# First mixer: the decays' chain reordered on every engine, norm powers in four pieces, masked product and last value tile moved

## The chip, the cores and the metric

One NeuronCore of a Trainium2 chip runs the whole program in one launch. The metric is the device time in microseconds, the median of the runs. The engines: TensorE (PE) multiplies, VectorE (DVE), ScalarE (ACT) and GpSimd (POOL) do elementwise work, SyncE (SP) issues the DMAs.

## What is computed

1024 tokens with 1024 features pass through a first block (a gated delta rule mixer, GDN, then a gated linear attention mixer, each with residual and layer norm) and a second one (windowed attention and sparse latent attention, then a feed-forward network). The change touches the GDN mixer only. It has 8 heads, keys of 128, values of 256, and works in chunks of 64 tokens:

```python
qkv = causal_conv_silu(p[..., :GDN_QKV], conv_w)        # p = x @ w_in, 4 taps, then silu
q, k = l2norm(q), l2norm(k)                             # t * rsqrt(sum(t*t) + 1e-6)
beta = sigmoid(b_logit); g = -exp(a_log) * softplus(a_logit + dt_bias)
gc = cumsum(g)                                          # within a chunk
decay = where(causal, exp(gc_i - gc_j), 0)
A = where(strict, (k*beta) k^T * decay, 0)
u, w = solve(A + I, [v*beta, k*beta*exp(gc)])           # unit lower triangular
qk = (q k^T) * decay
# scan over chunks: v_new = u - w S; o = (q*exp(gc)) S + qk v_new; S = S*g_last + k_dec^T v_new
# then o * rsqrt(mean(o*o) + 1e-6) * norm_w * silu(gate), and the product with w_out
```

## The kernel before

**Groups and tiles.** The mixer runs over 4 groups of 2 heads. A group projects 12 tiles of 128 output columns by 1024 tokens: 0 and 1 are q, 2 and 3 k, 4 to 7 v, 8 to 11 the gate. A tile is 48 matmuls of 128x512 (8 pieces of the contraction, 2 halves of the tokens, 3 products of high and low parts; `half`, lines 630, 631, 633). The raw weights of a tile come by DMA into one buffer; ScalarE rounds out the high part (`split`, line 1338), VectorE subtracts it for the low part (`split`, line 1951), and the next load waits for that. Two pairs of part buffers alternate, so the high part of tile i + 2 waits for the matmuls of tile i.

**Convolution.** ScalarE writes the first product from PSUM into one of two accumulators (`conv_first`, line 1352), VectorE adds three taps (`tap`, line 1962), ScalarE takes the silu (`conv_last`, line 1357). For q and k ScalarE squares (line 1361) and TensorE sums over the features by 8 products with one column of ones (`squares`, line 661), tile i into columns 8i to 8i + 7 of PSUM bank 6. For v TensorE turns the tile (`turn_values`, line 668) into the pair of banks 4 and 5, and VectorE scales it with beta into `vtok` (`values`, line 1969). For a gate tile ScalarE writes a silu (`gate`, line 1365).

**Scales.** When all four squares are there, VectorE's `scalars` adds 1e-6 (line 2008), GpSimd raises all 32 columns to -0.5 (line 2739), and VectorE makes the scales of A, of the keys and of the outputs (lines 2010 to 2016, event `sc`).

**Decays.** For each n of 8 pairs of chunks `decay` goes round the engines: GpSimd multiplies the triangle U with g (line 2667, `rU`); TensorE sums it over rows (line 692, `rB`); VectorE subtracts gc (line 2023, `rr`, which waits for `sc`); ScalarE takes exp (line 1410, `ex`); GpSimd zeroes the upper part (line 2672, `D`); TensorE has made k k^T and k q^T (lines 697, 699, `kk`); VectorE scales them (lines 2031, 2036: `B`, `qkT`); TensorE transposes B (line 707, `bT`), and ScalarE copies it, scaled, as A (lines 1420, 1421).

**Inverse.** `tee` inverts four n at a time by levels of masks: VectorE masks A (line 2047, `am` 0), writes I - that (line 2050) into `XX`, TensorE transposes it (line 721, `x0`), VectorE writes I - x0 (line 2054, `x1`); then for levels 1 to 6 TensorE multiplies the masked A (line 731), ScalarE copies the product into `Wb` (line 1432), TensorE multiplies again (lines 743, 745), and VectorE subtracts (lines 2063 to 2069). GpSimd makes the masked A of levels 1 to 5 (line 2686). TensorE uses banks 4 to 7 here. `XX` lies where accumulator 0 is; `Wb` and the mask buffer of even levels, `Am[0]`, lie where accumulator 1 is.

**Order.** Each engine has its own program, and an order is written out by hand: a yield is a place at which the other generator goes on. All engines follow the same two functions:

```python
def gdn_order(g, tiles, decay, tee, before_scan, scan_step):
    def four(q):
        for n in range(4 * q, 4 * q + 4):
            yield from decay(g, n)
    v_steps = tiles(g, range(5, 9))
    for _ in range(3):
        next(v_steps)
    interleave([four(0), v_steps])
    tee(g, 0)
    interleave([four(1), tiles(g, range(9, 12), True)])
    tee(g, 1)
```

`interleave` takes one step of each in turn until both are through. On TensorE `tiles` yields after 6, 9, 15 (9 and the 6 of the next half) and 9 matmuls of a tile, four times a tile; the convolution of tile i - 1 goes with the projection of tile i. `decay` yields four times for n < 4 and three times for n >= 4. `place_` takes the next PSUM bank of a ring and waits until its last tenant is emptied.

Of the kernel before, what the change touches and what calls it, by code (L numbers as in the profile page):

```python
# [166 lines left out]
def program(nc, I, out):  # L167
    ctx = ExitStack()
    with ctx:
# [86 lines left out]
        Am = [shared[:, 1536 + i * 512:2048 + i * 512] for i in range(2)]  # L256
# [4 lines left out]
        oT_odd = flat_masks[:, 448:960]  # L261
        sm = cutter(small, 832)
# [5 lines left out]
        rqk = sm(32)  # L268
# [201 lines left out]
        def gdn_order(g, tiles, decay, tee, before_scan, scan_step):  # L470
            def four(q):
                for n in range(4 * q, 4 * q + 4):
                    yield from decay(g, n)

            v_steps = tiles(g, range(5, 9))
            for _ in range(3):
                next(v_steps)
            interleave([four(0), v_steps])
            tee(g, 0)
            interleave([four(1), tiles(g, range(9, 12), True)])  # L480
            tee(g, 1)
            before_scan(g)
            for n in range(10):
                scan_step(g, n)
# [112 lines left out]
        def pe_program(e):  # L597
# [59 lines left out]
            def squares(g, i):  # L657
                sqb = bank[6]
                pe.wait_ge(("sq", g, i), ("ones",))
                for n in range(8):  # L660
                    m = mm(sqb[:, i * 8 + n:i * 8 + n + 1], accs[i % 2][:, n * 128:(n + 1) * 128], ones[:, 0:1], True, True)
                m.then_inc(*did("sqs", g, i))

            def turn_values(g, i):
                b = place_(R["v"], ("vT", g, i), ("v", g, i))
                pe.wait_ge(("s", g, i), ("ident",))
                for n in range(8):
                    m = tr(b[:, n * 128:(n + 1) * 128], accs[i % 2][:, n * 128:(n + 1) * 128], ident)
                m.then_inc(*did("vT", g, i))
# [18 lines left out]
            def decay(g, n):  # L688
# [13 lines left out]
                if n < 4:  # L702
                    yield
# [137 lines left out]
            for g in range(4):  # L841
                R["p"], R["v"], R["f"], R["r"] = Ring([1, 0] if g else [0, 1], True), Ring([2], True), Ring([0, 1]), Ring([6, 7])
                R["n"], R["k"] = Ring([4, 5]), Ring([2, 3])
                place_(Ring([6]), ("sqb", g), ("rqk", g))
# [476 lines left out]
        def act_program(e):  # L1321
# [45 lines left out]
            def tiles(g, some, last=False):  # L1367
                for i in some:
                    if i < 11:
                        split(12 * g + i + 1)  # L1370
                    if i - 1 < 8:
                        conv_first(g, i - 1)
                    else:
                        gate(g, i - 1)
                    yield from blank(4)
                    if i - 1 < 8:
                        conv_last(g, i - 1)
                    if i - 1 < 4:
                        square(g, i - 1)
                if last:  # L1380
                    gate(g, 11)
# [25 lines left out]
            def decay(g, n):  # L1407
# [4 lines left out]
                if n < 4:  # L1412
                    yield
# [11 lines left out]
            def tee(g, q):  # L1425
                ac.wait_ge([("vT", g, 6), ("vT", g, 7)] if q == 0 else None)
# [502 lines left out]
        def dve_program(e):  # L1929
# [42 lines left out]
            def tiles(g, some, _=False):  # L1972
                for i in some:
                    if i < 11:
                        split(12 * g + i + 1)
                    yield
                    for s_ in range(1, 4):
                        if i - 1 < 8:
                            tap(g, i - 1, s_)
                        yield  # L1980
                    if 4 <= i - 1 < 8:
                        values(g, i - 1)
# [20 lines left out]
            def scalars(g):  # L2003
# [3 lines left out]
                dv.wait_ge([("sqs", g, i) for i in range(4)], ended(g))  # L2007
                ts(rqk, bank[6][:, 0:32], 1e-6, None, ALU.add).then_inc(*did("rqk", g))
                dv.wait_ge(("rqp", g))
# [8 lines left out]
            def decay(g, n):  # L2018
# [20 lines left out]
                if n < 4:  # L2039
                    yield  # L2040

            def tee(g, q):
# [3 lines left out]
                dv.wait_ge([("A", g, n) for n in ns], ("d", "masks"), [("w", g, n - 4, 4) for n in ns] if q else [("vT", g, 6), ("vT", g, 7)])  # L2046
                tt(am, A8, tri[:, 0, :].unsqueeze(1).to_broadcast([128, 8, 64]), ALU.mult).then_inc(*did("am", g, q, 0))
                for c, n in enumerate(ns):
                    dv.wait_ge(("am", g, q, 0), ("xw", g, n - 4, 6) if q else None)
                    stt(XX[:, c, 0:2, :], am[:, 2 * c:2 * c + 2, :], -1.0, ident2.unsqueeze(1).to_broadcast([128, 2, 64]),  # L2050
                        ALU.mult, ALU.add).then_inc(*did("x0d", g, n))
                for c, n in enumerate(ns):
                    dv.wait_ge(("x0", g, n))
                    stt(XX[:, c, 2:4, :], at("x0", g, n)[:, 0:128].rearrange("p (j c) -> p j c", j=2), -1.0,
                        ident2.unsqueeze(1).to_broadcast([128, 2, 64]), ALU.mult, ALU.add).then_inc(*did("x1", g, n))
                for l in range(1, 7):
# [114 lines left out]
            for g in range(4):  # L2171
                if g == 0:
# [9 lines left out]
                    for s_ in range(1, 4):  # L2182
                        tap(0, 0, s_)
                        tap(0, 1, s_)
                    run(tiles(g, [3, 4]))
                    rates()
                    decays()
                else:
                    split(12 * g + 1)
                    for i in range(1, 5):  # L2190
                        split(12 * g + i + 1)
                        for s_ in range(1, 4):
                            tap(g, i - 1, s_)
                scalars(g)
                gdn_order(g, tiles, decay, tee, skip, scan_step)
# [437 lines left out]
        def pool_program(e):  # L2633
# [30 lines left out]
            def decay(g, n):  # L2664
# [3 lines left out]
                i_.then_inc(*did("rU", g, n))  # L2668
                yield
# [6 lines left out]
                if n < 4:  # L2676
                    yield

            def tee(g, q):
                ns = range(4 * q, 4 * q + 4)  # L2680
                A8 = kd_a.rearrange("p (x c) -> p x c", x=8)
                po.wait_ge([("A", g, n) for n in ns], ("d", "masks"), [("vT", g, 6), ("vT", g, 7)])
# [54 lines left out]
            for g in range(4):  # L2737
                po.wait_ge(("rqk", g))
                tt(rqk, rqk, cm05[:, 0:32], ALU.pow).then_inc(*did("rqp", g))
# [537 lines left out]
```

## Time and profile before

| | |
|---|---|
| median of 3 runs | 3395.48 us (3391.42 to 3397.43) |
| the profiled execution | 3392.56 us, span 3390.8 us |
| granted TensorE clock, mean | 0.978 |
| TensorE busy | 3214.0 us, 95% of the span |
| VectorE, ScalarE, GpSimd busy | 50%, 35%, 16% |
| group 1 of the first mixer | its first projection matmul starts at 323.80 us |

How to read it: on an engine, instructions run in the order of its program, and an instruction that waits holds up all behind it. Matmuls are pipelined: a 128x512 one is shown with 0.39 us and the next starts 0.23 us later. PEclk is the granted clock as a share of 2.4 GHz: 1.00 is 2.4 GHz, and at its lower level the engine runs at 1.2 GHz. The first groups differ from each other only at their start and end, so group 1 is shown for all.

### The profile page before, as it was taken

The numbers are of one execution on the slowest core, as the hardware profiler recorded it, in microseconds if no ns is written. First come the engines' busy times: TensorE is split into PE (matmuls) and PEld (weight loads), VectorE is DVE, ScalarE is ACT, GpSimd is POOL, SyncE is SP. The second block draws the span as 40 slices with busy tenths as digits, with TensorE's granted clock in tenths as the row PEclk, the third lists the DMA queues.
The fourth block names the chain that finished last, engine by engine and source line by source line (L and its number), as shares of the span: only waits on it lengthen the run. The fifth ranks groups of instructions, "written<-read, shape, count | busy, mean of one in ns | idle before, by whom it ended". The sixth has DMA issues, their size and how long they took to land.

```text
span 3390.8 us, 48503 instructions
## 1 busy us (share of the span) xinstructions
PE 3214.0 (95%) x19989; PEld 2658.8 (78%) x19989; DVE 1697.1 (50%) x3474; ACT 1202.8 (35%) x2403; POOL 533.8 (16%) x785
## 2 busy tenths in 40 slices
PE   8999999999999989899889999999999999999998
PEld 6778878877887767787767788778888788888886
DVE  3444445354444645545563799576643333234234
ACT  4442344244344433423353232466732311111113
POOL 0220112022012423203262132000110000000000
PEclk9999999999999989999989999999999999999999
DMA  2113102201220021132112132100042311111111
GB/s 103 38 39 114 42 20 76 87 27 44 100 87 33 32 72 51 49 104 88 53 65 77 38 106 82 56 1 1 1 174 100 131 38 62 38 50 50 50 50 50
DMA packets 59479, 210.12 MB, mean 62 GB/s; under 512 B 7015, under 2 KB 11721, under 8 KB 54522
## 3 DMA queue, kind: packets, MB, share of 16 engines
q1 hardware_dynamic: 59258, 207.02, 17.7%
q8 instruction: 157, 2.57, 0.3%
q14 instruction: 64, 0.52, 0.0%
HBM read 161.91 MB, written 45.09 MB: 61 GB/s over the span
## 4 chain that ended last, share of the span: by engine, by line
PE 85%; DVE 5%; ACT 4%; POOL 3%; issue 2%; DMA 1%; SPq 0%; POOLq 0%; DVEq 0%; ACTq 0%
PE pp L630 11%; PE pp L631 10%; PE pp L633 10%; PE pp L1237 9%; PE pp L1238 8%; PE pp L1239 8%; PE pp L803 2%; PE pp L805 2%; PE pp L804 2%; PE pp L1210 2%; PE pp L1194 2%; PE pp L731 1%; PE pp L761 1%; PE pp L745 1%; PE pp L743 1%
## 5 line engine op out<-in xcount | busy, mean ns | idle before, releaser
L630 PE MATMUL pp<-gx_hi,pw_hi 128*128 128x512 f32 x1504 | 617.0, 410 | 20.3 <-DVE pw_lo L1951 20.3
L633 PE MATMUL pp<-gx_hi,pw_lo 128*128 128x512 f32 x1504 | 595.8, 396 | 0.0
L631 PE MATMUL pp<-gx_lo,pw_hi 128*128 128x512 f32 x1504 | 594.8, 396 | 0.0
L630 PEld LDWEIGHTS pp<-gx_hi,pw_hi 128*128 128x128 f32 x1504 | 288.0, 191 | 86.0 <-DVE pw_lo L1951 20.7
L633 PEld LDWEIGHTS pp<-gx_hi,pw_lo 128*128 128x128 f32 x1504 | 287.2, 191 | 63.2
L631 PEld LDWEIGHTS pp<-gx_lo,pw_hi 128*128 128x128 f32 x1504 | 287.9, 191 | 55.4
L1237 PE MATMUL pp<-mix_hi,wt_hi 128*128 128x512 f32 x704 | 274.1, 389 | 2.8 <-DVE arena L2596 1.6
L1238 PE MATMUL pp<-mix_lo,wt_hi 128*128 128x512 f32 x704 | 273.9, 389 | 0.0
L1239 PE MATMUL pp<-mix_hi,wt_lo 128*128 128x512 f32 x672 | 261.4, 389 | 0.0
L1924 ACT ACTIVATE xT<-pp 128x1024 f32<-128x1024 f32 x22 | 22.6, 1029 | 535.4 <-PE pp L1239 535.4
L2628 DVE TENSOR_TENSOR xT<-xT,pp 128x1024 f32<-128x1024 f32 x22 | 26.9, 1221 | 368.8 <-ACT xT L1924 368.8
L1951 DVE TENSOR_TENSOR pw_lo<-arena,pw_hi 128x1024 fp32r<-128x1024 f32 x68 | 83.6, 1230 | 231.3 <-ACT pw_hi L1338 231.3
L1237 PEld LDWEIGHTS pp<-mix_hi,wt_hi 128*128 128x128 f32 x704 | 132.1, 188 | 30.6 <-DVE arena L2596 1.8
L1238 PEld LDWEIGHTS pp<-mix_lo,wt_hi 128*128 128x128 f32 x704 | 132.1, 188 | 27.4
L1239 PEld LDWEIGHTS pp<-mix_hi,wt_lo 128*128 128x128 f32 x672 | 126.1, 188 | 26.2
L2615 DVE TENSOR_TENSOR y_ffn<-y_ffn,pp 128x512 f32<-128x512 f32 x176 | 115.7, 684 | 57.3 <-PE pp L1239 56.5
L2886 POOL TENSOR_SCALAR small<-small 128x1 f32<-128x1 f32 x16 | 3.0, 190 | 821.9 <-ACT xT L1846 723.1
L1237 PE MATMUL pp<-wt_hi,a_hi 128*128 128x512 f32 x336 | 132.1, 393 | 0.0
L1238 PE MATMUL pp<-wt_lo,a_hi 128*128 128x512 f32 x336 | 131.0, 390 | 0.0
L1239 PE MATMUL pp<-wt_hi,a_lo 128*128 128x512 f32 x336 | 130.8, 389 | 0.0
L2421 DVE TENSOR_SCALAR_CACHE_REDUCE xT<-y,small 128x656 bf16<-128x656 f32 (+1 forms) x124 | 128.5, 1092 | 0.0
L1338 ACT ACTIVATE pw_hi<-arena 128x1024 fp32r<-128x1024 f32 x68 | 71.6, 1054 | 156.4 <-PE pp L633 119.2
(507 smaller groups left out, 6808.9 us busy)
## 6 DMA issues: line engine op xcount, KB each, us to landing
arena<-in_tiles_dram SPq DMA_DIRECT2D x73, 512.0 KB, 3.6
arena<-in_units_dram SPq DMA_DIRECT2D x33, 1024.0 KB, 4.8
y_scratch<-y SPq DMA_DIRECT2D x48, 512.0 KB, 2.9
y<-y_scratch SPq DMA_DIRECT2D x40, 512.0 KB, 4.6
xT<-in_tiles_dram SPq DMA_DIRECT2D x27, 512.0 KB, 4.0
xT<-in_w_outs_dram SPq DMA_DIRECT2D x12, 1024.0 KB, 7.2
arena<-gates_scratch SPq DMA_DIRECT2D x16, 512.0 KB, 3.4
xT<-in_wall_dram SPq DMA_DIRECT2D x3, 2048.0 KB, 10.0
```

Source lines behind the costliest of these rows:

```text
L630: mm(b[:, hs], wh[:, c], X[0][:, k, hs], k == 0, False)
L631: m = mm(b[:, hs], wh[:, c], X[1][:, k, hs], False, both and k == 7)
L633: m = mm(b[:, hs], wl[:, c], X[0][:, k, hs], False, k == 7)
L803: mm(b, hi[:, t, :], wh, t == 0, False)
L804: mm(b, hi[:, t, :], wl, False, False)
L1237: mm(o, l[0][:, c], r[0][:, d], first, False)
L1238: mm(o, l[0][:, c], r[1][:, d], False, False)
L1239: return mm(o, l[1][:, c], r[0][:, d], False, last)
L1338: act(parts(u)[0], tile_place[u], ACT.Copy).then_inc(*did("ph", u))
L1951: tt(lo, tile_place[u], hi.bitcast(F32), ALU.subtract).then_inc(*did("pl", u))
L2421: i_ = ts(vis[i], work[i], thr[:, i - 1:i] if bit < 31 else 0.0, None, ALU.is_ge, ALU.add, accum_out=count[:, i - 1:i])
L2615: tt(yv, yv, at("dn", j, n, hf), ALU.add).then_inc(*did("yd", j, n, hf))
```

## The change

- The powers of the norms are made by tiles: VectorE's `norm_piece` adds 1e-6 to 8 columns, GpSimd's `power` raises 8 columns, and `scales` (the rest of `scalars`) is called in `gdn_order` after the first three steps of the value tiles. The squares of tile i lie in bank 6 + i % 2. GpSimd's `sums` for n = 0 (line 2667) is made ahead of the fourth power.
- `decay` has the additional yield for n < 2 only, on all four engines.
- `Am[0]` lies in the second half of the masks' buffer (the place of `oT_odd`, used in the scan), so the masked product waits for A and no longer for the value tiles.
- The last value tile is turned into the ring of the projections; VectorE scales value tile 6 one step later, in the next tile's first step, and tile 7 in `tee` behind line 2054.
- VectorE makes the low parts of tiles 9, 10 and 11 after the first yield of a tile instead of ahead of it.
- ScalarE makes gate tile 8 and the high part of tile 10 at the head of `tee` instead of behind it, and the silu of tile 7 one step earlier.

```diff
 Wb = shared[:, 1024:1536].rearrange("p (c e) -> p c e", c=4)
-Am = [shared[:, 1536 + i * 512:2048 + i * 512] for i in range(2)]
 halves = (slice(0, 64), slice(64, 128))
...
 oT_odd = flat_masks[:, 448:960]
+Am = [oT_odd, shared[:, 2048:2560]]
 sm = cutter(small, 832)
...
-def gdn_order(g, tiles, decay, tee, before_scan, scan_step):
+def gdn_order(g, tiles, decay, tee, before_scan, scan_step, scales=None):
     def four(q):
...
         next(v_steps)
+    if scales:
+        scales(g)
     interleave([four(0), v_steps])
...
     def squares(g, i):
-        sqb = bank[6]
+        sqb = place_(Ring([6 + i % 2]), ("sqs", g, i), ("rqk", g, i))
         pe.wait_ge(("sq", g, i), ("ones",))
...
     def turn_values(g, i):
-        b = place_(R["v"], ("vT", g, i), ("v", g, i))
+        b = place_(R["p" if i == 7 else "v"], ("vT", g, i), ("v", g, i))
         pe.wait_ge(("s", g, i), ("ident",))
...
         yield
-        if n < 4:
+        if n < 2:
             yield
...
         R["n"], R["k"] = Ring([4, 5]), Ring([2, 3])
-        place_(Ring([6]), ("sqb", g), ("rqk", g))
         R["d"] = Ring([6, 7])
...
     def tiles(g, some, last=False):
         for i in some:
-            if i < 11:
+            if i < 11 and i != 9:
                 split(12 * g + i + 1)
...
                 conv_first(g, i - 1)
-            else:
+            elif i != 9:
                 gate(g, i - 1)
-            yield from blank(4)
+            yield from blank(3 if i == 8 else 4)
             if i - 1 < 8:
...
         yield
-        if n < 4:
+        if n < 2:
             yield
...
     def tee(g, q):
-        ac.wait_ge([("vT", g, 6), ("vT", g, 7)] if q == 0 else None)
+        if q == 0:
+            gate(g, 8)
+            split(12 * g + 10)
+            ac.wait_ge(("vT", g, 6), ("vT", g, 7))
         for l in range(1, 7):
...
     def tiles(g, some, _=False):
         for i in some:
-            if i < 11:
+            if i < 8:
                 split(12 * g + i + 1)
             yield
+            if i == 8:
+                values(g, 6)
+            if 8 <= i < 11:
+                split(12 * g + i + 1)
             for s_ in range(1, 4):
...
                 yield
-            if 4 <= i - 1 < 8:
+            if 4 <= i - 1 < 6:
                 values(g, i - 1)
...
     def rates():
...
-    def scalars(g):
+    def norm_piece(g, i):
+        c = slice(8 * i, 8 * i + 8)
+        dv.wait_ge(("sqs", g, i), ended(g))
+        ts(rqk[:, c], at("sqs", g, i)[:, c], 1e-6, None, ALU.add).then_inc(*did("rqk", g, i))
+
+    def scales(g):
         def two(a):
...
-        dv.wait_ge([("sqs", g, i) for i in range(4)], ended(g))
-        ts(rqk, bank[6][:, 0:32], 1e-6, None, ALU.add).then_inc(*did("rqk", g))
-        dv.wait_ge(("rqp", g))
+        dv.wait_ge([("rqp", g, i) for i in range(4)])
         ts(rqk[:, 0:16], rqk[:, 0:16], 128.0 ** -0.5, None, ALU.mult).then_inc(*did("rqs", g))
...
         yield
-        if n < 4:
+        if n < 2:
             yield
...
     def tee(g, q):
...
         A8 = kd_a.rearrange("p (x c) -> p x c", x=8)
-        dv.wait_ge([("A", g, n) for n in ns], ("d", "masks"), [("w", g, n - 4, 4) for n in ns] if q else [("vT", g, 6), ("vT", g, 7)])
+        dv.wait_ge([("A", g, n) for n in ns], ("d", "masks"), [("w", g, n - 4, 4) for n in ns] if q else ended(g))
         tt(am, A8, tri[:, 0, :].unsqueeze(1).to_broadcast([128, 8, 64]), ALU.mult).then_inc(*did("am", g, q, 0))
         for c, n in enumerate(ns):
-            dv.wait_ge(("am", g, q, 0), ("xw", g, n - 4, 6) if q else None)
+            dv.wait_ge(("am", g, q, 0), ("xw", g, n - 4, 6) if q else ("vT", g, 6))
             stt(XX[:, c, 0:2, :], am[:, 2 * c:2 * c + 2, :], -1.0, ident2.unsqueeze(1).to_broadcast([128, 2, 64]),
...
                 ident2.unsqueeze(1).to_broadcast([128, 2, 64]), ALU.mult, ALU.add).then_inc(*did("x1", g, n))
+        if q == 0:
+            values(g, 7)
         for l in range(1, 7):
...
                 tap(0, 1, s_)
+            norm_piece(g, 0)
+            norm_piece(g, 1)
             run(tiles(g, [3, 4]))
+            norm_piece(g, 2)
             rates()
+            norm_piece(g, 3)
             decays()
...
                 split(12 * g + i + 1)
+                if i >= 2:
+                    norm_piece(g, i - 2)
                 for s_ in range(1, 4):
                     tap(g, i - 1, s_)
-        scalars(g)
-        gdn_order(g, tiles, decay, tee, skip, scan_step)
+        if g:
+            norm_piece(g, 3)
+        gdn_order(g, tiles, decay, tee, skip, scan_step, scales)
...
-    def decay(g, n):
+    def sums(g, n):
         po.wait_ge(("gg",), ("U",), ("bT", g, n - 1) if n else ended(g))
...
         i_.then_inc(*did("rU", g, n))
+
+    def power(g, i):
+        c = slice(8 * i, 8 * i + 8)
+        po.wait_ge(("rqk", g, i))
+        tt(rqk[:, c], rqk[:, c], cm05[:, c], ALU.pow).then_inc(*did("rqp", g, i))
+
+    def decay(g, n):
+        if n:
+            sums(g, n)
         yield
...
         yield
-        if n < 4:
+        if n < 2:
             yield
...
     def tee(g, q):
...
         A8 = kd_a.rearrange("p (x c) -> p x c", x=8)
-        po.wait_ge([("A", g, n) for n in ns], ("d", "masks"), [("vT", g, 6), ("vT", g, 7)])
+        po.wait_ge([("A", g, n) for n in ns], ("d", "masks"), ended(g))
         for l in range(1, 6):
...
     for g in range(4):
-        po.wait_ge(("rqk", g))
-        tt(rqk, rqk, cm05[:, 0:32], ALU.pow).then_inc(*did("rqp", g))
+        for i in range(3):
+            power(g, i)
+        sums(g, 0)
+        power(g, 3)
         gdn_order(g, lambda g_, some, last=False: blank(4 * len(some)), decay, tee, skip, scan_step)
```

## Rows read from the trace of the kernel before

**Rows 1.** The page, busy time of each engine (share of the span) and instructions

```profile
PE 3214.0 (95%) x19989; PEld 2658.8 (78%) x19989; DVE 1697.1 (50%) x3474; ACT 1202.8 (35%) x2403; POOL 533.8 (16%) x785
```

**Rows 2.** TensorE's waits, 0 to 1130 us: us in total, times, longest

```profile
PE pp L707 <- DVE arena L2031: 14.6, 8, 1.9
...
PE pp L721 <- DVE arena L2047: 10.0, 4, 2.5
PE pp L668 <- ACT arena L1357: 8.8, 4, 2.2
...
PE pp L692 <- POOL arena L2667: 1.2, 1, 1.2
```

**Rows 3.** Timeline of TensorE, group 1, start of decays: start us, length us

```profile
383.74 1.84 PE L661 MATMUL pp<-consts,arena 128*128 128x1 f32 x16
...
392.65 0.67 PE L692 MATMUL pp<-arena,consts 128*128 128x256 f32 x2
...
397.95 0.39 PE L633 MATMUL pp<-gx_hi,pw_lo 128*128 128x512 f32 x1
400.56 1.09 PE L668 MATMUL pp<-consts,arena 128*128 128x128 f32 x8 [2.23 <-ACT arena L1357]
```

**Rows 4.** Timelines of the other engines in the same stretch

```profile
378.54 1.06 ACT L1361 ACTIVATE arena<-arena 128x1024 f32<-128x1024 f32 x1
...
385.89 5.42 POOL L2739 TENSOR_TENSOR small<-small,consts 128x32 f32<-128x32 f32 x1 [73.38 <-DVE small L2008]
...
393.27 3.90 DVE L1962 SCALAR_TENSOR_TENSOR arena<-pp,small,arena 128x1023 f32<-128x1023 f32 x3
...
398.16 1.28 ACT L1357 ACT_TABLE_LOAD   x1
399.45 1.06 ACT L1357 ACTIVATE arena<-arena 128x1024 f32<-128x1024 f32 x1
```

**Rows 5.** GpSimd's groups by form, whole run: busy us, mean ns

```profile
L2660 POOL TENSOR_TENSOR small<-small,consts 128x8 f32<-128x8 f32 x2 | 3.3, 1672 | 0.2
```

**Rows 6.** Timeline of VectorE, group 1, ahead of the first inverse

```profile
443.56 1.22 DVE L1969 TENSOR_TENSOR arena<-pp,small 128x1024 f32<-128x1024 f32 x1 [5.30 <-PE pp L668]
444.70 0.60 DVE L2031 SCALAR_TENSOR_TENSOR arena<-pp,small,arena 128x128 f32<-128x128 f32 x2
```

**Rows 7.** Timeline of TensorE, group 1, start of the first inverse

```profile
442.49 1.04 PE L668 MATMUL pp<-consts,arena 128*128 128x128 f32 x8
445.45 0.41 PE L707 MATMUL pp<-consts,arena 128*128 128x128 f32 x2 [1.92 <-DVE arena L2031]
448.35 1.97 PE L721 MATMUL pp<-consts,arena 64*64 64x64 f32 x32 [2.49 <-DVE arena L2047]
450.43 1.97 PE L731 MATMUL pp<-arena 64*64 64x64 f32 x32
...
454.37 1.14 PE L731 MATMUL pp<-arena 64*64 64x64 f32 x32
...
457.21 1.14 PE L731 MATMUL pp<-arena 64*64 64x64 f32 x32
```

**Rows 8.** Timeline of ScalarE, group 1, behind the first inverse

```profile
469.56 1.01 ACT L1365 ACTIVATE xT<-pp 128x1024 f32<-128x1024 f32 x1
```

**Rows 9.** The page, DMA issues: KB each, median us to landing

```profile
arena<-in_tiles_dram SPq DMA_DIRECT2D x73, 512.0 KB, 3.6
```

**Rows 10.** Busy time in stretches: PE PEld DVE ACT POOL, PEclk, DMA share, GB/s

```profile
402.00:406.00 4.00, 4.00 (x12) 3.13 (x12) 4.00 (x7) 0.46 (x1) 0.00 (x0) 0.61 0.24 59
...
985.00:990.00 5.00, 5.00 (x20) 4.12 (x18) 4.12 (x7) 1.47 (x2) 0.00 (x0) 0.66 0.13 26
...
690.00:700.00 10.00, 7.82 (x41) 6.22 (x40) 5.96 (x10) 6.52 (x12) 1.60 (x3) 1.00 0.17 54
```

**Rows 11.** Timelines, group 1, fifth decay step

```profile
486.10 1.23 DVE L1951 TENSOR_TENSOR pw_lo<-arena,pw_hi 128x1024 fp32r<-128x1024 f32 x1 [5.57 <-ACT pw_hi L1338]
...
487.99 0.41 PE L707 MATMUL pp<-consts,arena 128*128 128x128 f32 x2 [1.72 <-DVE arena L2031]
```


## The prediction

> **What bounds the kernel now.** I read the page's busy times first: TensorE is busy for 95% of the span [rows 1], so only time in which it stands still, or runs at the lower clock, can be won. Next the waits of TensorE over the first mixer (0 to 1130 us of the trace), longest first [rows 2]: the transposes of the decay matrices (line 707) waited 14.6 us in 8 places for VectorE's line 2031, the first product of the inverse (line 721) 10.0 us in 4 places for line 2047, the value transposes (line 668) 8.8 us in 4 places for ScalarE's silu, and line 692 once, 1.2 us, for GpSimd. That is 34.6 us, in the same three places in each of the four groups (group 0 has the 1.2 besides). Everything between these places is back to back. The reader is to see that each place is a chain through other engines that begins too late, not an engine without capacity; the timelines of group 1 show which link is late.
>
> **Place 1, the start of the decays.** TensorE issues its last matmul of tile 5 at 397.95 and the value transpose only at 400.56 [rows 3]. With the pace of 0.23 us per matmul, 2.38 us are lost from issue to issue (the wait of 2.23 is counted from the modelled end). Back along the chain [rows 4]: the silu at 399.45 follows a table load of 1.28 us, and this follows exp and subtraction behind the three taps of VectorE that began at 393.27, which were queued behind the scales, which waited for the power on GpSimd, 5.42 us from 385.89. **The change** cuts the power into four pieces of 8 columns. A power of that shape takes 1.67 us [rows 5], against 5.42 for 32 columns. Three pieces run while tiles are still projected, and the last starts at about 385.9. VectorE does the split and two taps of tile 4 before it waits for it: from 385.7, 1.2 and 2.6 us, thus 389.5, by when the power (387.6) is done; were a piece as dear as the whole it would be done at 391.3, still early enough. So the scales are no longer in front of the taps' data. What is late next is the first row sum of the decays, which TensorE issues at 392.65 [rows 3] in its own order and has at 393.3: subtraction and exp 1.0 (from the taps' end at 397.17 to the table load at 398.16 [rows 4]), table load 1.28, silu 1.06, thus about 396.6, against 398.2, when TensorE wants it. The stall goes with 1.6 us to spare. **Gain: 4 x 2.38 = 9.5 us.** In group 0 the row sum also waits for its multiplied mask on GpSimd, behind the power: 1.2 by the wait, 1.3 from issue to issue. The mask now goes before the last power. Against it stands one new hop: the fourth piece's bank is the one that the cumulative sums (line 654) use next, so they wait for VectorE's small addition. No row shows that hop; it lies between 0 and the 0.60 us of a pair of VectorE operations on 256 columns [rows 6]; I take 0.4, as a single addition on 8 columns is nearer to the upper end only by its two handovers. Net 0.9.
>
> In every group VectorE now also waits for the squares before the taps of the next tile. The squares hold TensorE for 1.84 us [rows 3] behind the tile's last matmul, while the taps in any case wait for ScalarE's first product, a pass like the square's 1.06 us [rows 4]; a tap chain starts up to 1 us later. Cover: the square of tile 3 ends at 379.6 [rows 4], 4.1 us before TensorE asks for it at 383.74. Costed at nothing; without that cover it would be 1 us a tile, 12 us in all.
>
> **Place 2, the start of the inverse.** In group 1 [rows 7] the transposes of the last value tile begin at 442.49 and take 0.88 to issue (to 443.37); then 445.45 the last decay transpose, 448.35 line 721, 450.43 the first line 731. So 7.06 us pass between the value tile and line 731. Why [rows 6]: VectorE did the last value tile (1.22 us at 443.56) ahead of line 2031 at 444.70, and the transpose waited for that; behind the transpose come the scaled copies on ScalarE and the masked product on VectorE. **The change** shortens the chain by one step for n = 2 and 3 (14 steps for 14 pieces of TensorE's tiles instead of 16), so the last decay transpose is issued before the last 9 matmuls and the value transposes; it puts the last value tile behind line 2054, and the masked product into a buffer that does not wait for the values. Chain from the decay transpose to line 731: 450.43 - 445.45 = 4.98 us, which I keep. TensorE now fills the first 0.24 + 9 x 0.227 + 0.88 = 3.16 us of it. The value tile to line 731 is then 4.98 - 3.16 = 1.82 us, and the transpose's 0.24 lies in front: 7.06 - 1.82 - 0.24 = **5.0 us a group, 20.0 us**. Of the 1.82, 1.0 is line 721's own work and 0.8 a stall that stays.
>
> The covers, counted from the end of tile 7: value transposes 0.9, values 6 on VectorE until 2.5, split until 3.6, taps until 8.0 with line 2023 of n = 3 between them, line 2031 at 8.6; TensorE asks for it at 11.4. Silu 7 is done at 9.6 and needed at 13.7. The mask of n = 3 on GpSimd needs 1.2 us after a transpose and has 2.0. On ScalarE the gate of tile 8 and the high part of tile 10 now stand ahead of the inverse's copies, about 1 us each, as gate 8's 1.01 [rows 8]: from the end of tile 8 (13.9) until 15.9, and the first copy is wanted at 16.9. Tile 10's load is issued once the low part of tile 9 is there (3.6), and lands in 3.6 us [rows 9], at about 7.5. VectorE's last value tile, 1.22 us behind line 2054, ends about 0.2 us after the first product wants its subtraction; the next round absorbs that. Bank 4 to 7: the last value tile now sits in the tiles' pair, so tile 9 waits for gate 8 (done 15.0, wanted after 40), tile 10 for values 7 and tile 11 for gate 9, all early.
>
> **The clock.** After this stall line 721 and the first line 731 take 1.97 us instead of the 1.14 of the next, and from the first to the second round 3.94 us pass, against 2.84 from the second to the third [rows 7]: 1.1 us a group at half clock. If TensorE works on, **4.4 us** come back. In groups 1 and 3 the granted clock also fell behind place 1, to 0.61 over 4 us and 0.66 over 5 us [rows 10]: 4 x 0.39 and 5 x 0.34, **3.2 us**. Bounds for both together: nothing (it falls elsewhere) to 7.6. I take them whole, as each fall follows a stall that goes. But group 2 had the same stall in 690 to 700 us and kept a clock of 1.00 [rows 10]: whether a stall costs the clock is chance. The Trainium skill (TensorE: Matmul & The Clock Gate, "Part 1: The HAM clock gate") says that a monitor sets the clock by how busy the array was recently, on a count of its own that doesn't start anew with the kernel. By that rule a stall elsewhere can meet a bad moment as well after the change, and the sum would be smaller by the 3.2; by it the trace's one group without a fall beside two with one is as expected.
>
> **Place 3, the fifth decay step.** TensorE waited 1.72 us before 487.99 [rows 11]; with the 0.16 us by which a matmul's modelled end lies behind the issue of the next (0.39 against 0.23), 1.88 us lost. VectorE's line 2031 stood behind the split of tile 11 (486.10 [rows 11]), which waits for ScalarE's high part and this for tile 9's end. In the new order VectorE does each split of these tiles after the first yield, thus behind line 2031. The copies of ScalarE stay behind gate 9 as before, and TensorE's next decay transpose comes 7 us later. **4 x 1.88 = 7.5 us.** No edit touches SyncE's program; its tile loads follow the low parts, at most 1.2 us later each, against the 11 us of a tile's 48 matmuls.
>
> **Sum.** 9.5 + 0.9 + 20.0 + 4.4 + 3.2 + 7.5 = 45.5 us. The profiled execution took 3392.6 us, the median of the runs is 2.9 above it. 3392.6 - 45.5 = 3347.1, as a median 3350. The rest of the kernel (from about 1085 us on) is the same instructions and moves as a block.
>
> **Rivals.**
> - *The clock does not come back (0.13).* The 0.8 us that stay, followed by thin 64x64 products, could leave the half-clock stretch where it is. For: the rows show it right there. Against: the third round, with the same thin products, runs at full speed [rows 7]. Gain 45.5 - 7.6 = 37.9: 3358.
> - *The short steps are too short (0.17).* For n = 2 and 3 there is one piece of TensorE less between the row sum and the transpose. If exp and silu with their table loads, or GpSimd's mask, are late, place 2 gives up about 2.5 us a group, and some stall comes in the middle: 45.5 - 10 - 2 = 33.5: 3362.
> - *Slower (0.04).* The inverse's copies now stand behind the high part of tile 10 on ScalarE, which waits for that tile's load. Place: between gate 8 and line 1432. The load has 14.9 - 3.6 = 11.3 us. Beyond that each us costs one in each group; from 23 us on the whole 45.5 are gone (4 x 11.4), and with 25 us it would be 3403. Against: loads land in 3.6 us, in the median.
> - *It does nothing that counts (0.04).* The gains are taken back in the scan, if that waits for loads or rows: 3395. Against: no such wait over 1 us in TensorE's list.
>
> **Numbers.** Forecast 0.62, rivals as given. Faster by over 0.2% (6.8 us, about what a measurement of this kernel can tell from no change) 0.92, within it 0.04, slower 0.04. Low end: the 0.8 us stalls go too (3.2), and the half-clock stretch at the end of the inverse shrinks, some 6 us: 3340. High end: both middle rivals in part together, 3371.
>
> **What would show it.** Right: in TensorE's waits lines 707 and 668 gone, line 721 gone and in its place about 0.8 us before line 731 in each group; four small powers of about 1.7 us per group; line 731 of the first round in 1.1 us. Wrong: a wait of line 707 for line 2031 in the first four steps (second rival), clock of 0.7 at the inverse's start (first), or ScalarE's line 1338 waiting for a load before the inverse (third).

## The result

The changed kernel takes 3352.0 us (3351.6 to 3355.1), against 3393.8 us for the kernel before on the same chips: a ratio of 0.9879 (95% interval 0.9865 to 0.9893), 41.8 us. The forecast was 3350, the range 3340 to 3371. The profiled executions have spans of 3390.8 and 3350.0 us, 40.8 us apart, against 45.5 worked out. "Before" and "after" below are these two profiles; the other runs are named by what they undo.

TensorE's waits in the first mixer (0 to 1110 us; us in total, times, longest), which answer to [rows 2]:

```profile
PE pp L632 <- DVE pw_lo L1955: 14.4, 1, 14.4
PE pp L736 <- DVE arena L2080: 7.6, 23, 0.4
...
PE pp L733 <- DVE arena L2065: 2.2, 4, 0.6
...
PE pp L656 <- DVE small L2014: 0.3, 1, 0.3
```

The lines that led [rows 2] are gone: no wait of 709 (707 before), 723 (721), 670 (668) or 694 (692) is left. New are 0.56 us before the first line 733 in each group, and the hop of group 0 at line 656, 0.26 us. What waits besides (line 736 at the inverse's last level, the weights of tile 0) waited before as well.

The start of the decays in group 1, timelines of TensorE, GpSimd, VectorE and ScalarE (start, length), for [rows 3] and [rows 4]:

```profile
389.00 0.39 PE L635 MATMUL pp<-gx_hi,pw_lo 128*128 128x512 f32 x1
389.23 1.03 PE L670 MATMUL pp<-consts,arena 128*128 128x128 f32 x8
...
377.24 2.58 POOL L2693 TENSOR_TENSOR small<-small,consts 128x8 f32<-128x8 f32 x1 [9.30 <-DVE small L2014]
...
377.07 1.22 DVE L1955 TENSOR_TENSOR pw_lo<-arena,pw_hi 128x1024 fp32r<-128x1024 f32 x1
378.21 2.60 DVE L1966 SCALAR_TENSOR_TENSOR arena<-pp,small,arena 128x1023 f32<-128x1023 f32 x2
380.73 0.17 DVE L2021 TENSOR_SCALAR small<-small 128x16 f32<-128x16 f32 x1
...
386.77 1.06 ACT L1358 ACTIVATE arena<-arena 128x1024 f32<-128x1024 f32 x1
```

The value transpose follows the last matmul at the ordinary 0.23 us. The silu ends at 387.8, 1.4 us before it. The first scale (line 2021) comes right behind the second tap, so the last power costs VectorE nothing.

The start of the inverse in group 1, for [rows 6] and [rows 7]:

```profile
427.64 0.38 PE L709 MATMUL pp<-consts,arena 128*128 128x128 f32 x2
...
429.93 1.03 PE L670 MATMUL pp<-consts,arena 128*128 128x128 f32 x8
430.90 1.15 PE L723 MATMUL pp<-consts,masks 64*64 64x64 f32 x32
432.61 1.15 PE L733 MATMUL pp<-arena 64*64 64x64 f32 x32 [0.56 <-DVE arena L2065]
435.45 1.14 PE L733 MATMUL pp<-arena,masks 64*64 64x64 f32 x32
...
428.06 0.63 ACT L1421 ACTIVATE arena<-pp,small 64x64 f32<-64x64 f32 x2 [2.68 <-PE pp L709]
...
430.13 1.02 ACT L1366 ACTIVATE xT<-pp 128x1024 f32<-128x1024 f32 x1 [0.39 <-PE pp L635]
431.18 1.06 ACT L1339 ACTIVATE pw_hi<-arena 128x1024 fp32r<-128x1024 f32 x1
433.16 0.92 ACT L1436 ACTIVATE arena<-pp 128x128 f32<-128x128 f32 x4 [0.92 <-PE pp L733]
```

From the value transposes' start to line 733 it is now 2.68 us, where it was 7.94. The last decay transpose (427.64) now stands ahead of the last 9 matmuls and the value transposes, and from it to line 733 it is 4.97 us, the 4.98 that the forecast kept. The copies of the last decay matrix begin 1.9 us before the value transposes, so the chain runs under them. Line 733 takes 1.15 us instead of 1.97, and the next round comes 2.84 us later instead of 3.94: the half-clock stretch is away. Tile 10's high part (431.18) didn't wait for its load.

**Where the 40.8 us come from.** Each group cut at the starts of named instructions (first row sum of n = 0; first x0 product of the first inverse; row sum of n = 4; x0 of the second inverse; first key transpose; tile 0 of the next group), in us, before and after:

| stage | group 0 | group 1 | group 2 | group 3 | gain |
|---|---|---|---|---|---|
| start to row sum | 100.74, 101.76 | 68.85, 68.59 | 68.86, 68.59 | 68.86, 68.59 | -0.2 |
| to first inverse | 54.12, 47.12 | 55.70, 47.14 | 54.11, 47.10 | 55.71, 47.13 | 31.2 |
| first inverse | 20.73, 19.29 | 20.77, 19.28 | 20.29, 19.29 | 20.61, 19.28 | 5.3 |
| to second inverse | 42.95, 39.64 | 42.96, 39.55 | 42.91, 41.13 | 42.94, 41.07 | 10.4 |
| second inverse and scan | 105.26, 107.36 | 104.49, 104.06 | 105.06, 108.02 | 116.29, 117.38 | -5.7 |

What follows takes 2178.6 us in both; that they agree so closely is in part luck, as the same changed kernel took 2174.2 and 2175.3 us there in its other two profiles. The last row is a loss in stages that no edit touches. In group 1, where no fall of the clock came, the scan alone (from the first key transpose) takes 84.61 us in both kernels. The busy time by stretches (PE, PEld, DVE, ACT, POOL, then the granted clock) shows why; the first fence is the changed kernel, the second the one before at about the same work:

```profile
230.00:240.00 10.00, 8.46 (x32) 5.98 (x31) 3.39 (x8) 3.63 (x10) 1.69 (x4) 0.78 0.00 0
790.00:800.00 10.00, 9.11 (x33) 6.52 (x31) 2.98 (x8) 4.12 (x13) 2.87 (x4) 0.66 0.00 0
1070.00:1080.00 10.00, 8.52 (x92) 6.49 (x88) 4.07 (x16) 4.25 (x11) 4.99 (x4) 0.71 0.01 2
```

```profile
240.00:250.00 10.00, 8.45 (x41) 6.34 (x40) 4.77 (x11) 4.53 (x13) 2.93 (x5) 1.00 0.00 0
820.00:830.00 10.00, 8.12 (x61) 6.07 (x56) 5.12 (x16) 5.32 (x17) 4.59 (x6) 1.00 0.00 0
1110.00:1120.00 10.00, 8.14 (x152) 6.85 (x149) 4.94 (x19) 5.35 (x15) 6.86 (x6) 1.00 0.02 4
```

The clock of TensorE fell to its lower level at the start of three scans, where it had held before. No stall as long as those of the three places stands in front of these falls: in the 3 us before the first one TensorE's longest wait was 0.37 us, at the inverse's last level (line 736), and from 228 us on the clock was at 1.2 GHz:

```profile
224.00:227.00 3.00, 2.02 (x48) 1.61 (x45) 2.54 (x10) 1.12 (x4) 2.36 (x2) 1.00 0.02 5
228.00:231.00 3.00, 2.69 (x8) 1.46 (x6) 0.28 (x1) 1.42 (x4) 2.50 (x2) 0.50 0.00 0
```

In the first row of the table, group 0 lost 1.0 us, with one fall more than before (the stretch of 90 to 100 us has a clock of 0.83, before 1.00). Groups 1 to 3 gained 0.26 us each, which the forecast didn't have: the mask for the row sum stood behind the power there too (GpSimd was through with it at 392.51, TensorE's row sum came at 392.65).

### The profile page after: what moved, and what is told of

It reads as the page before. It is cut to its first block, busy times and chain, and to the rows that moved or that the text cites. A ratio compares the mean times of both kernels' runs of the same rounds, so it can differ in the third digit from the quotient of the medians.

```text
span 3350.0 us, 48536 instructions
## 1 busy us (share of the span) xinstructions
PE 3205.6 (96%) x19989; PEld 2651.2 (79%) x19989; DVE 1698.0 (51%) x3486; ACT 1203.4 (36%) x2403; POOL 548.2 (16%) x797
## 4 chain that ended last, share of the span: by engine, by line
PE 88%; DVE 4%; ACT 4%; POOL 2%; issue 1%; DMA 1%; SPq 0%; POOLq 0%; DVEq 0%; ACTq 0%
PE pp L632 11%; PE pp L633 11%; PE pp L635 11%; PE pp L1238 9%; PE pp L1239 9%; PE pp L1240 9%; PE pp L805 2%; PE pp L807 2%; PE pp L806 2%; PE pp L1211 2%; PE pp L1195 2%; PE pp L763 1%; PE pp L733 1%; PE pp L747 1%; PE pp L1203 1%
```

## The experiments

### Is the loss in the scans chance? The same kernel again, twice

No edit.

> The changed kernel as it is, once more. Theory A (the missing 5 us of the forecast are half-clock stretches that fall on the start of a group's scan by chance of the moment): the stretches of the other profile (2.2 us lost in 230 to 240, 3.4 in 790 to 800, 2.9 in 1070 to 1080) lie elsewhere or are longer or shorter by 1 to 3 us in all, and the stages without such a stretch agree to 0.1 us. Theory B (they belong to the new order itself, since the scan now begins sooner behind the second inverse): the same stages show the same stretches again.

Measured: 3352.8 us (3344.3 to 3359.1), profiled at a span of 3342.5. The stretches of the first fence above, in this profile:

```profile
230.00:240.00 10.00, 8.89 (x42) 7.08 (x43) 6.00 (x13) 5.05 (x16) 1.71 (x4) 1.00 0.00 0
790.00:800.00 10.00, 8.46 (x41) 6.32 (x40) 4.67 (x11) 4.64 (x13) 3.03 (x5) 1.00 0.00 0
1070.00:1080.00 10.00, 8.36 (x56) 6.10 (x54) 4.54 (x14) 5.39 (x16) 4.51 (x6) 1.00 0.00 0
```

> The changed kernel as it is beside the run above, for the comparison on the same chip: 3350 to 3354. In its profile the stretches at half clock are once more in other stages than in the first two; every stage without one keeps its length to 0.1 us.

Measured: 3354.0 us (3350.2 to 3362.9), profiled at 3348.5. The scans (from the first key transpose on) of groups 0 to 3 in the three profiles of one kernel:

| profile | group 0 | group 1 | group 2 | group 3 |
|---|---|---|---|---|
| first | 87.05 | 84.60 | 87.55 | 96.63 |
| again | 84.63 | 84.63 | 84.63 | 95.74 |
| third | 84.66 | 84.59 | 87.24 | 96.68 |

To the first inverse it is 47.10 to 47.14 us in all twelve groups, and the first inverse takes 19.28 to 19.42, while a scan of groups 0 to 2 takes 84.6 us without a fall and 87.1 to 87.6 with one, and the stretch to the second inverse 39.6 or 41.1. So a fall at one of these places comes in one execution and stays away in another, as theory A has it. The third profile met its own expectation only in part: its falls in the scans of groups 2 and 3 are at the places of the first profile's. The part that wanted every stage without a fall to agree to 0.1 us doesn't hold for the second inverse, which took 19.5 to 20.9 us without a fall (22.0 to 22.5 with one). There the trace also shows waits of TensorE put down to "issue", 0.8 to 2.2 us each, once in each group, in the kernel before too.

One question stays open. The kernel before has one profile, without a fall in the scans of groups 0 to 2; the eleven profiles of the changed kernel and its variants have one in 21 of 33 such scans. That the place is chance is shown; whether the new order makes such falls more frequent (a weaker form of theory B) is not settled, and would need more profiles of the kernel before.

### The same with TensorE 1.8 us later

```diff
                 for n in range(8):
                     m = mm(b[:, n * 16:(n + 1) * 16], baT[:, n * 128:(n + 1) * 128], ident2[:, 0:16], True, True)
+                for n in range(8):
+                    m = mm(b[:, n * 16:(n + 1) * 16], baT[:, n * 128:(n + 1) * 128], ident2[:, 0:16], True, True)
```

> Line 650's eight small products are made twice in group 0, with the same result: TensorE works about 1.8 us more at 81 us, and everything behind comes that much later. Theory A (chance of the moment): the half-clock stretches behind it move to other stages, and the sum changes by 1.8 us plus or minus 2 to 5 us. Theory B (they belong to the order): the same stages show them and the time rises by 1.8 us.

Measured: 3356.2 us (3355.2 to 3363.5), span 3353.5. The scans took 87.46, 87.58, 86.97 and 98.36 us, a fall in every group. This doesn't tell the theories apart: falls came at the places of the first profile and at one more. Since unchanged runs vary as much, the 3.4 us over the changed kernel on the same chip (3352.8) can't be split between the work and the clock.

### Place 3 alone undone: low parts before the yield

```diff
-                    if i < 8:
+                    if i < 11:
                         split(12 * g + i + 1)
                     yield
                     if i == 8:
                         values(g, 6)
-                    if 8 <= i < 11:
-                        split(12 * g + i + 1)
```

> VectorE makes the low parts of tiles 9 to 11 before the first yield again; all else as changed. Theory A (line 2031 stood behind the split of tile 11): TensorE's wait of 1.7 us for VectorE's line B in the fifth decay step comes back in each group, 7.5 us from issue to issue, 3359. Rival: the two chains merely overlap and the earlier start of exp behind the gate already brought this gain: no wait, 3352.

Measured: 3357.5 us (3357.1 to 3360.3), 0.9895 (0.9880 to 0.9910). TensorE's waits of this kernel:

```profile
PE pp L632 <- DVE pw_lo L1955: 13.7, 1, 13.7
PE pp L709 <- DVE arena L2040: 10.1, 8, 1.7
```

Four of the eight are the 1.72 us of the fifth step, as forecast. The other four are 0.81 us each at n = 3: the low part of tile 9 also moved, and it delays the last line 2040 of the first batch. To the first inverse it is 48.0 us instead of 47.1, to the second 41.3 (42.9 in group 0, with a fall) instead of 39.6. So this edit is worth 4 x (0.9 + 1.7) = 10.4 us by the stages (by accident the number of the stage's gain above, which holds 7.5 of stall and 2.9 of clock), though the medians on this chip are only 4.7 us apart and the intervals of the two ratios overlap. Its four executions had a granted clock of 0.981 to 0.983, those of the changed kernel beside it 0.978 to 0.984, with three of the four at or under 0.980.

### Place 2, one half undone: long steps for n = 2 and 3

```diff
-                if n < 2:
+                if n < 4:
                     yield
```

on all four engines.

> Decay steps 2 and 3 get their additional yield back on all four engines; all else as changed. Theory A: the last decay transpose again stands behind the last value transposes; the wait for B itself stays away since value tile 7 no longer stands before it on VectorE, but the chain of 4.98 us from this transpose to line 733 lies bare, where 3.16 us of it were covered: 12.6 us in four groups, and about 4 us more at half clock: 3369. Rival (the moved value tile and mask buffer alone brought the gain): under 4 us, 3355.

Measured: 3366.9 us (3364.4 to 3367.7), 0.9920 (0.9905 to 0.9934), 14.1 us slower than the changed kernel on the same chip (3352.8). Its TensorE, group 1:

```profile
433.84 1.03 PE L670 MATMUL pp<-consts,arena 128*128 128x128 f32 x8
434.71 0.38 PE L709 MATMUL pp<-consts,arena 128*128 128x128 f32 x2
437.59 1.97 PE L723 MATMUL pp<-consts,masks 64*64 64x64 f32 x32 [2.49 <-DVE masks L2058]
439.67 1.98 PE L733 MATMUL pp<-arena 64*64 64x64 f32 x32
```

The transpose doesn't wait any longer, as the value tile has left its way, and from it to line 733 it is 4.96 us: the chain that the sum kept at 4.98. The half clock is back behind the 2.49 us here and in groups 0 and 2; in group 3 the same wait was followed by no fall, and the inverse took 19.7 us.

### Place 2, the other half undone: value tile 7 before the mask

```diff
-        Am = [oT_odd, shared[:, 2048:2560]]
+        Am = [shared[:, 1536:2048], shared[:, 2048:2560]]
...
-                b = place_(R["p" if i == 7 else "v"], ("vT", g, i), ("v", g, i))
+                b = place_(R["v"], ("vT", g, i), ("v", g, i))
...
-                    if 4 <= i - 1 < 6:
+                    if 4 <= i - 1 < 6 or i == 8:
                         values(g, i - 1)
...
-                if q == 0:
-                    values(g, 7)
```

and both masked products wait for the value transposes again.

> Only the third part is undone: the masked product lies over accumulator 1 again and waits for the value transposes, value tile 7 is turned into banks 4 and 5 and scaled on VectorE before the mask; the shorter steps and the rest stay. Theory A: the mask product waits for value tile 7, about 2.3 us later than now in each group, 9 us, and up to 4 us at half clock: 3361 to 3365. Rival (the shorter steps alone brought the gain): under 2 us, 3353.

Measured: 3358.8 us (3352.2 to 3361.5), 0.9896 (0.9882 to 0.9911).

```profile
430.78 1.03 PE L670 MATMUL pp<-consts,arena 128*128 128x128 f32 x8
433.84 1.15 PE L723 MATMUL pp<-consts,arena 64*64 64x64 f32 x32 [2.03 <-DVE arena L2058]
434.98 1.59 PE L733 MATMUL pp<-arena 64*64 64x64 f32 x32
```

Line 723 waits 2.0 us, and to the first inverse it is 49.2 us (47.1); the first inverse itself takes 20.1 (19.3). A fall of the clock stands in the inverse of all four groups. That is 4 x 2.9 = 11.6 us by the stages, 6.8 by the medians, whose intervals overlap, so the stages carry this reading. Before the inverse the long steps gave back 2.4 us a group (49.5 against 47.1) and this edit 2.1: each half brings about half of the gain there. No run undid both at once.

### Place 1: pieces, place of the scales, both

One power, scales late:

```diff
-                for i in range(3):
-                    power(g, i)
                 sums(g, 0)
-                power(g, 3)
+                po.wait_ge([("rqk", g, i) for i in range(4)])
+                tt(rqk, rqk, cm05[:, 0:32], ALU.pow).then_inc(*did("rqp", g, 3))
```

and VectorE waits for this one power.

> The power is again one instruction of 32 columns (5.42 us), the additions by pieces and the scales behind two taps stay. Theory A (the place of the scales brought the gain, the pieces add nothing): the power ends at about 391.3 us by group 1's old times, the third tap ends 1.5 us later than now but before the row sum is used; no wait at the value transposes, 3352. Rival (the pieces are what counts): the wait of 2.2 us comes back, 3361.

Measured: 3354.4 us (3352.3 to 3356.9), 0.9887 (0.9872 to 0.9902); 47.1 us to the first inverse in all groups, no wait at line 670.

Pieces, scales ahead of the taps:

```diff
-            v_steps = tiles(g, range(5, 9))
-            for _ in range(3):
-                next(v_steps)
             if scales:
                 scales(g)
+            v_steps = tiles(g, range(5, 9))
+            for _ in range(3):
+                next(v_steps)
```

> Powers by pieces stay, but the scales stand ahead of the split and the taps again. Theory A (either of the two edits is enough, as the row sum is what is late next): the last power of about 1.7 us delays the taps by about 2 us, which the 1.6 us to spare behind the row sum and the 1.8 us before it hold: no wait at the value transposes, 3352. Rival (the place of the scales alone counts): a wait of 1 to 2 us in each group, 3356 to 3360.

Measured: 3349.1 us (3344.3 to 3354.9), 0.9872 (0.9857 to 0.9886); 47.1 us again, no wait.

Both edits together:

> One power of 32 columns and the scales ahead of the taps: place 1 is undone as a whole, apart from the mask of n = 0, made before the power. Theory A: the wait of 2.2 us at the value transposes is back in all four groups, 9.5 us from issue to issue, up to 3 us more at half clock: 3361 to 3365. If this is under 4 us, place 1 was not worth what the forecast gave it.

Measured: 3364.7 us (3363.0 to 3366.0), 0.9915 (0.9899 to 0.9932).

```profile
PE pp L632 <- DVE pw_lo L1955: 14.4, 1, 14.4
PE pp L670 <- ACT arena L1358: 9.1, 4, 2.5
```

The stall is back only when both are undone: each edit alone takes the delay out, since the row sum of n = 0 is late next. 12.7 us over the changed kernel: 9.1 of waiting and, in three groups, a fall of the clock behind it (51.2 to 51.4 us to the first inverse, where group 0 has 49.0).

The edits add up. To the first inverse, without a fall, undoing costs a group 1.9 us for place 1 (group 0), 2.4 and 2.1 for the halves of place 2 and 0.9 for the low parts, 7.3 together; the two kernels are 7.0 us apart there in groups 0 and 2.

### What is left: the 0.56 us before line 733

```diff
-                        pe.wait_ge(("we", g, n, l))
+                        pe.wait_ge(("we", g, n, l), ("x0d", g, n) if l == 1 else None)
...
                 for c, n in enumerate(ns):
+                    dv.wait_ge(("x0", g, n), ("xw", g, n - 4, 6) if q else ("vT", g, 6))
+                    stt(XX[:, c, 2:4, :], at("x0", g, n)[:, 0:128].rearrange("p (j c) -> p j c", j=2), -1.0,
+                        ident2.unsqueeze(1).to_broadcast([128, 2, 64]), ALU.mult, ALU.add).then_inc(*did("x1", g, n))
+                for c, n in enumerate(ns):
-                    dv.wait_ge(("am", g, q, 0), ("xw", g, n - 4, 6) if q else ("vT", g, 6))
+                    dv.wait_ge(("am", g, q, 0))
                     stt(XX[:, c, 0:2, :], am[:, 2 * c:2 * c + 2, :], -1.0, ident2.unsqueeze(1).to_broadcast([128, 2, 64]),
                         ALU.mult, ALU.add).then_inc(*did("x0d", g, n))
-                for c, n in enumerate(ns):
-                    dv.wait_ge(("x0", g, n))
-                    stt(XX[:, c, 2:4, :], at("x0", g, n)[:, 0:128].rearrange("p (j c) -> p j c", j=2), -1.0,
-                        ident2.unsqueeze(1).to_broadcast([128, 2, 64]), ALU.mult, ALU.add).then_inc(*did("x1", g, n))
...
-                        dv.wait_ge(("xw", g, n, l), ("xu", g, n, l - 1) if l > 1 else ("x1", g, n))
+                        dv.wait_ge(("xw", g, n, l), ("xu", g, n, l - 1) if l > 1 else ("x0d", g, n))
```

> In both inverses VectorE writes the four line 2065 results (I - x0) before the four line 2061 results (I - masked A); TensorE's second products of level 1 wait for the latter besides. Theory: the first line 733 of a group waits 0.56 us for VectorE's line 2065, which stands behind four instructions of 0.46 us that only the second product needs; this wait goes, the stretch from the first line 723 to the second batch's first row sum falls from 19.3 to 18.6 to 18.8 us, 2 to 3 us in four groups: 3350. Rival: the products behind it then wait for line 2061 instead, and the stretch stays at 19.3 us.

Measured: 3351.5 us (3344.6 to 3357.6), 0.9868 (0.9851 to 0.9884), beside 0.9882 (0.9868 to 0.9896) for the changed kernel on the same chip: not to be told apart as a time. Timelines of VectorE and GpSimd, group 1 (lines 2061 and 2065 have changed their parts):

```profile
431.06 0.69 DVE L2058 TENSOR_TENSOR masks<-arena,masks 128x512 f32<-128x512 f32 x1 [2.86 <-ACT arena L1422]
432.69 0.99 DVE L2061 SCALAR_TENSOR_TENSOR arena<-pp,masks 128x128 f32<-128x128 f32 x4 [0.93 <-PE pp L723]
433.60 0.89 DVE L2065 SCALAR_TENSOR_TENSOR arena<-masks 128x128 f32<-128x128 f32 x4
...
431.11 1.77 POOL L2715 TENSOR_TENSOR arena<-arena,masks 128x512 f32<-128x512 f32 x1 [6.30 <-ACT arena L1422]
```

The wait is gone and the first inverse takes 18.85 us in each group instead of 19.29: 1.8 us in four groups, by the trace, under the lower end of what was expected. Line 733 follows line 723 at once.

## Why the prediction was right, and where it was off

- **The three places and their links** were right. To the first inverse the working gives 9.5 (place 1) + 4 x 4.65 (the part of place 2 before line 723) + 3.2 (clock behind place 1) = 31.3 us, and 31.2 were measured. The undoings bear out the parts (7.3 against 7.0 us a group). The first inverse: 4 x 0.35 + 4.4 = 5.8, measured 5.3. How near the time came (3350 against 3352.0) is better than the working: the gain was put 3.7 us too high (45.5 against 41.8 by the medians), and 1.7 us of that are taken back by the median it starts from, 3395.5 of three runs, where four gave 3393.8.
- **"Were a piece as dear as the whole ... still early enough"** was tested directly by the single late power, and holds. The forecast didn't see that the pieces alone are enough as well.
- **Spare times**: silu ready 1.4 us early instead of 1.6; stall before line 733 0.56 us, 0.7 from issue to issue, instead of 0.8; the hop in group 0 0.26 us of waiting instead of 0.4. The net 0.9 of group 0 didn't show in the changed kernel's profile (its stretch to the row sum grew by 1.0, with a fall more); the kernel with place 1 undone, which keeps the early mask and has no such fall, has 100.07 there against 100.74 before, so about 0.7.
- **Place 3** was put at 7.5 us and its stage gave 10.4. The stall went as said. The 2.9 us above it are two falls of the clock behind the first inverse, which the kernel before had in all four groups and this profile in groups 2 and 3 only. The forecast's clock term didn't hold these at all, although its trace had them. They are no lasting gain either: the third profile of the changed kernel has this fall in all four groups.
- **The step that was off** is "I take them whole, as each fall follows a stall that goes", of the clock's 7.6 us. Those two places did give it back, but as an account of the kernel the term is wrong: falls went from the two places named and two more, and new ones came at the scans (-5.7 us with the second inverse) and in group 0's start, where the stretch of 90 to 100 us has a clock of 0.83. Those at the scans followed no stall over 0.4 us, so taking stalls away doesn't take them away. Nor does a stall of place 1 always bring one: it did in groups 1 and 3 and didn't in groups 0 and 2, where the prediction counted one group without. Three profiles of one kernel differ by 7.5 us in span, 3.1 of them up to the end of the first mixer's fourth group and 4.4 behind it. The sum without any clock term, 37.9, and the one with it, 45.5, stand on both sides of the 40.8 measured; that the sum came out within 5 us is in this term luck.
- **The rivals**: the short steps were not too short, and the high part of tile 10 waited for no load. The first rival's mechanism (the 0.6 us that stay and the thin products keep the half clock at the inverse) didn't occur with the change; low clock at the inverse's start came back only behind waits of 2.0 and 2.5 us, in seven of eight groups. The fourth rival asked for waits in the scan: a scan without a fall takes 84.6 us in both kernels, so the loss there is the clock's alone.

## What to carry to other kernels

On an engine that is busy for 95%, ask for each of its stalls which single instruction was queued ahead of the late one on the feeding engine, and whether that instruction had to be there; the chain's length itself seldom has to change. When two edits aim at one stall, undo each by itself and both together: here either was enough at one place, and at another each brought about half. Cut a profile at fixed instructions and compare stages: where the clock didn't fall, most of them repeated to 0.1 us (the second inverse to 1.4) and priced edits of 2 to 10 us, where single executions of the changed kernel ran from 3344 to 3363 us. Count a fall of the clock as won only when several profiles lack it.

## What the hardware showed besides

- **GpSimd and VectorE hold each other up.** The last power took 2.58 us beside VectorE's split (377.07 to 378.29), and 1.66 us in the kernel with the scales first, where VectorE idled. The power began 0.17 us behind the split; waiting for its end and then working 1.67 us gives 2.7, 0.1 more than measured. In the other direction, VectorE's four I - masked A took 1.85 us beside GpSimd's masked product and 0.89 us in the last experiment, where they came behind it (first fence: the changed kernel; second: the one with the scales first):

```profile
429.82 1.77 POOL L2715 TENSOR_TENSOR arena<-arena,masks 128x512 f32<-128x512 f32 x1 [6.33 <-ACT arena L1422]
430.50 1.85 DVE L2061 SCALAR_TENSOR_TENSOR arena<-masks 128x128 f32<-128x128 f32 x4
```

```profile
379.50 1.66 POOL L2693 TENSOR_TENSOR small<-small,consts 128x8 f32<-128x8 f32 x1 [9.30 <-DVE small L2014]
```

The Trainium skill (SBUF — State Buffer, "Who interferes with whom") says that a VectorE instruction with two SBUF inputs contends with a GpSimd instruction that reads SBUF, that the port pair they share is an exclusive lock, and that the order of issue decides who blocks. These traces agree: the later of the two was the longer one both times, by about what was left of the earlier. The forecast's 1.67 us for a power had no such neighbour.

- **A GpSimd power costs by the column**: 5.42 us for 32 columns, 1.66 for 8, undisturbed. Cutting it in four cost 16 x 1.82 = 29.0 us of GpSimd against 21.7, all of it off the path.
